# The first memory value panel of a two-block transformer kernel, in four pieces instead of two at the start of the second attention

## The reference

```python
h = x @ w_in[l]
o_a = mla_mixer(cq, ckv, kr, ...)          # 8 heads, latent attention, causal
o_b = nsa_mixer(nq, kc, vc, ks, vs, kw, vw, gl, ...)
#     8 heads, three branches: 15 compressed keys, selected blocks, window
x = layer_norm(ALPHA * x + concat([o_a, o_b]) @ w_out[l], ...)
k, v = split(memn @ xa_wkv[l], 2)          # memory keys and values, 256 x 1024 each
x = layer_norm(ALPHA * x + softmax(q @ k.T) @ v @ xa_wo[l], ...)
x = layer_norm(ALPHA * x + conv_ffn(x), ...)
```

## Time and profile before

| | |
|---|---|
| runs | 1833.0, 1834.21, 1839.84 us; median 1834.21 |
| the profiled execution | 1841.68 us; its span 1839.8 us |
| TensorE (PE) busy | 1771.1 us, 96% of the span |
| VectorE (DVE) | 1058.2 us, 58% |
| ScalarE (ACT) | 355.3 us, 19% |
| GpSimd (POOL) | 190.8 us, 10% |
| mean granted clock of TensorE | 0.979 of full speed |
| start of the second attention | 892.12 us in layer 1, 1421.54 us in layer 2 |

### The profile page before, as it was taken

How to read it: one execution, slowest core, us unless ns; L and a number is a source line. 1 busy time by engine, 2 the same in 40 slices (tenths; PEclk the granted TensorE clock), 3 DMA queues, 4 the chain that set the end, 5 groups by cost and what they waited for, 6 DMA issues and landing times.

```text
span 1839.8 us, 22077 instructions
## 1 busy us (share of the span) xinstructions
PE 1771.1 (96%) x8510; PEld 1307.5 (71%) x8510; DVE 1058.2 (58%) x2084; ACT 355.3 (19%) x881; POOL 190.8 (10%) x126
## 2 busy tenths in 40 slices
PE   7999999998899999999999999999999999999997
PEld 6886488744747885477694859984668766689953
DVE  6766468524654776641172158995712451369985
ACT  1111000132401111102270212220012440222210
POOL 1212212000011122120001000002110000000010
PEclk9999999999899999999989999999999899999999
DMA  9644354523066454436303435453355105164440
GB/s 319 209 138 177 120 206 135 192 102 115 8 207 198 150 178 160 161 104 194 148 15 125 138 115 168 155 182 133 138 143 203 72 1 199 52 204 154 170 160 23
DMA packets 162502, 265.59 MB, mean 144 GB/s; under 512 B 4008, under 2 KB 105684, under 8 KB 162270
## 3 DMA queue, kind: packets, MB, share of 16 engines
q1 hardware_dynamic: 157470, 248.18, 40.1%
q0 software_dynamic: 4768, 15.48, 2.5%
q10 hardware_dynamic: 160, 0.52, 0.1%
HBM read 262.56 MB, written 1.08 MB: 143 GB/s over the span
## 4 chain that ended last, share of the span: by engine, by line
PE 76%; DVE 14%; DVEq 4%; ACT 3%; issue 2%; DMA 1%; SPq 1%; ACTq 0%
PE psum L764 14%; PE psum L924 11%; PE psum L820 10%; PE psum L737 8%; PE psum L1125 5%; PE psum L1042 4%; PE psum L1077 3%; PE psum L1336 3%; PE psum L1293 3%; PE psum L714 3%; DVE work L2354 3%; PE psum L975 2%; PE psum L963 2%; DVE ring L1865 2%; PE psum L1059 2%
## 5 line engine op out<-in xcount | busy, mean ns | idle before, releaser
L608 POOL TENSOR_TENSOR work<-ring,work 128x1024 f32<-128x1024 f32 (+1 forms) x57 | 141.4, 2482 | 809.5 <-DVE work L1867 809.5
L924 PE MATMUL psum<-ring,work 128*128 128x512 f32 x352 | 161.9, 595 | 3.4 <-DVE work L2387 3.4
L1863 DVE TENSOR_TENSOR work<-ring 128x1024 f32<-128x1024 f32 (+1 forms) x83 | 100.7, 1213 | 86.6 <-PE psum L924 80.8
L737 PE MATMUL psum<-ring,x_t 128*128 128x512 f32 x320 | 140.0, 595 | 7.4 <-ACT x_t L1394 7.4
L924 PEld LDWEIGHTS psum<-ring,work 128*128 128x128 f32 x352 | 66.5, 190 | 85.0 <-issue 79.9
L924 PE MATMUL psum<-work 128*128 128x512 f32 x264 | 123.3, 596 | 0.0
L737 PEld LDWEIGHTS psum<-ring,x_t 128*128 128x128 f32 x320 | 60.0, 190 | 81.5 <-issue 71.8
L2007 DVE CUSTOM_DVE_ANT_0 work<-psum,work 128x256 f32<-128x256 f32 (+1 forms) x96 | 31.3, 364 | 131.2 <-PE psum L1042 131.2
L1865 DVE TENSOR_TENSOR ring<-ring 128x1024 f32<-128x1024 f32 (+1 forms) x83 | 102.3, 1232 | 6.2
L1867 DVE TENSOR_TENSOR work<-ring 128x1024 f32<-128x1024 f32 (+1 forms) x83 | 99.6, 1200 | 6.2
L924 PEld LDWEIGHTS psum<-work 128*128 128x128 f32 x264 | 50.1, 192 | 63.1 <-issue 61.4
(11 more groups left out here) (252 smaller groups left out, 2899.5 us busy)
## 6 DMA issues: line engine op xcount, KB each, us to landing
ring<-in_ffn_w_up_dram SPq DMA_DIRECT2D x66, 1024.0 KB, 7.9
ring<-in_w_in_dram SPq DMA_DIRECT2D x21, 2048.0 KB, 7.9
ring<-in_ffn_w_down_dram SPq DMA_DIRECT2D x20, 2048.0 KB, 7.8
ring<-in_ffn_w_gate_dram SPq DMA_DIRECT2D x22, 1024.0 KB, 5.5
ring<-in_xa_wkv_dram SPq DMA_DIRECT2D x8, 2048.0 KB, 7.9
ring<-in_w_out_dram SPq DMA_DIRECT2D x6, 2048.0 KB, 8.7
ring<-in_xa_wq_dram SPq DMA_DIRECT2D x4, 2048.0 KB, 7.8
ring<-in_xa_wo_dram SPq DMA_DIRECT2D x4, 2048.0 KB, 9.6
```

What stands on the lines that cost most here:

```text
L608: nc.gpsimd.tensor_tensor(t4, quarters(n, chunks, pitch)[2], t2, ALU.subtract).then_inc(fourth_ready, 1)
L737: return mm(bank(banks[2 * i + h]), acts[:, c, i * P:(i + 1) * P], ring[:, (n0 + c // 4) % RING, o:o + 512], start=(c == 0), stop=(c == KD ...
L924: last = mm(sums[p], acts[p][:, q, :], rhs[:, i, :], start=(q == 0), stop=(q == KF // 2 - 1))
L1863: v.tensor_tensor(t3, b22, b12, ALU.subtract)
```

## The change

The same sixteen products are issued in four groups of four: tile 0 with k = 0 to 3 before the scores of unit 1, tile 0 with k = 4 to 7 before those of unit 2, and tile 1 likewise before those of units 3 and 4. The wait of `keys_out` now stands ahead of the first group. `start` and `stop` still hold at k = 0 and k = 7, so an accumulation stays open in its bank while other banks are written. `panel_done` is raised by the last group, and ScalarE copies the two banks at its step 5.

```diff
-                def memory_values(j, tiles, banks):
+                def memory_values(j, tiles, banks, chunks=range(KD)):
 
                     n = at(L_WV[j], N_LAYER, l)
-                    if 0 in tiles:
+                    if 0 in tiles and 0 in chunks:
                         arrived(n)
                     for i in tiles:
-                        for k in range(KD):
+                        for k in chunks:
                             last = mm(bank(banks[i]), MEMT[:, k, i * P:(i + 1) * P], ring[:, n % RING, k * 512:k * 512 + 512],
                                       start=(k == 0), stop=(k == KD - 1))
-                    if 1 in tiles:
+                    if 1 in tiles and KD - 1 in chunks:
                         last.then_inc(panel_done, 1)
 
-                def keys_out():
-                    pe.wait_ge(group_free, at(H_WK + 2, G_LAYER, l))
-
-                def first_values():
-                    memory_values(0, (0,), (1, 3))
-
-                def second_values():
-                    memory_values(0, (1,), (1, 3))
+                def values_between(i, half):
+
+                    def between():
+                        if (i, half) == (0, 0):
+                            pe.wait_ge(group_free, at(H_WK + 2, G_LAYER, l))
+                        memory_values(0, (i,), (1, 3), range(4 * half, 4 * half + 4))
+                    return between
...
-                attend(UNITS_2, U1, l, {1: keys_out, 2: first_values, 3: second_values})
+                attend(UNITS_2, U1, l, {1 + 2 * i + h: values_between(i, h) for i in range(TT) for h in range(2)})
...
-                attend(UNITS_2, U1, l, {4: lambda: memory_values(0, (1, 3), 2)})
+                attend(UNITS_2, U1, l, {5: lambda: memory_values(0, (1, 3), 2)})
```

## The result

| | before | after |
|---|---|---|
| median of 16 runs each | 1835.09 us | 1825.21 us |
| lowest and highest | 1828.43, 1844.35 | 1816.31, 1830.6 |
| the profiled execution | 1841.68 us | 1828.62 us |
| its span | 1839.8 us | 1826.8 us |
| mean granted clock in it | 0.979 | 0.988 |

The ratio of the run times is 0.9937, with a 95% interval of 0.992 to 0.9955: the kernel is 0.6% faster. The chain of waits has not changed its shape (compare): TensorE is still 76% of it.

The account below looks back on a forecast made before the run. TensorE, 76% of the chain of waits, was taken as the bound. 6.2 + 1.7 + 4.0 + 1.5 - 2.0 = 11.4 us, 2.0 less in a median run, gave 9.4 off 1834.21: 1824.8 us, range 1818 to 1834.5.

Parts of the forecast that it names:

- First fall: Scores of units 0 and 1 and first half panel, both layers: parting the scores keeps the clock full; 6.2 us gained.
- The wait and the values behind it: Before and in unit 2's turn and unit 1's values: fourth group covers the wait, 1.7 us; clock stays full, 4.0 us.
- Units 5 to 13: Start of attention proper, both layers: VectorE and ScalarE set 1.51 us per unit at full clock; 1.5 us gained.
- Against it: Thin work after third and fourth groups: one clock fall in two layers and a little of a second; 2.0 us lost.
- From one execution to the median: Whole run: a median run has shorter clock falls than the profiled one, so the gain is 2.0 us less.
- Costs of nothing: Around the groups: earlier panel and keys' copy, later scores, panel copy one step on and next load cost nothing.
- the first: Moved stretch, both layers: clock holds throughout, gain 11.4 to 13.4 us, time 1821 to 1823; chance 0.22.
- Rival 3: Same stretch: slow time only moves, only the wait's 1.7 us is gained, 1832.5 us; chance 0.11.
- Rival 4: Panel pieces run at 1.2 GHz, each 3.43 us dearer; with five slow, 10 us slower, 1844; chance 0.07.

Follow-up runs that it names:

- e4: Kernel before plus four redundant products per layer between the scores of units 0 and 1: 1838.38 against 1838.01 us, ratio 1.0005.
- e8: The change measured again with no edit: 1822.98 us, ratio 0.9929 to the kernel before.
- e5: The change with ScalarE's panel copy at step 4 instead of 5: ratio 0.9932 to the kernel before.
- e10: The change with groups of 1, 7, 4 and 4 products before units 1 to 4: 1826.19 us, ratio 0.9945 to the kernel before.
- e3: The change regrouped as two groups of eight, before the scores of units 1 and 4: ratio 0.9984 to the kernel before.
- e9: The change with groups of 2, 6, 4 and 4 products before units 1 to 4: 1822.11 us, ratio 0.9924 to the kernel before.
- e7: The change with 4, 2, 3, 3 products before units 1 to 4, one each before 6, 8, 10, 12, copy at step 17: 1816.98 us, ratio 0.9901.

## Why the prediction was right

The mechanism was the forecast one. That the time is met to 0.5 us is in part luck, as the last two terms show. Step by step, measured in the profiled executions:

- **First fall**, 6.2 us expected. Scores 0 to 2 took 13.97 and 13.95 us before (892.12 to 906.09 in layer 1) and 10.94 after: 6.0. The clock held, as forecast, and e4 shows that it is the clock. The first two groups took 3.63 and 3.54 us from start to start instead of the 3.43 I took, and the scores of a unit 1.89 instead of 2.0.
- **The wait and the values behind it**, 1.7 + 4.0 us expected. From the scores of unit 2 to those of unit 5 it was 16.90 us (906.09 to 922.99) and 17.02; it is 14.30 in both: 5.3. In each layer the fourth group is 0.1 us longer than 3.43, and the turn of unit 2 takes 0.31 us instead of 0.22. The prediction's words that the clock falls "not after idleness" are shown for the first fall only; the second came right behind a wait.
- **Units 5 to 13**, 1.5 us expected, 2.8 measured (12.95 and 12.73 against 11.28 and 11.63). This term was mis-sized. I took VectorE's pace of 1.51 us for all eight units, but the first ones run at TensorE's 1.1 to 1.2 us until the other engines are the ones behind.
- **Against it**, 2.0 us expected for a fall left over. This term was mis-sized too. There was one fall in the profiled execution, in layer 2, but it met units 6 and 7 and not a piece of the panel. It cost nothing that can be read: layer 2's stretch takes 36.87 us with it and 36.86 in e8 without.
- **From one execution to the median**, 2.0 us expected. The profiled execution of before lies 6.6 us over the median of its kernel (1841.68 against 1835.09), that of the change 3.4 over its own (1828.62 against 1825.21): 3.2 us. Why is open. I put it down to shorter falls in this stretch in a median run, and no trace of a median run of before shows them.
- **Costs of nothing.** The two that were measured held: there is no wait before piece 1, and the copy's place is free (e5).

So 13.4 - 2.0 - 2.0 = 9.4 us was forecast, and what was measured is 14.1 in the two stretches, less 1.1 in the rest of the program and 3.2 from execution to median, which is 9.9 but for rounding. The gain in the stretches was put 2.7 us too low, and what had to come off it again 2.3 too low. The two errors cancel.

Of the rivals, the first (the clock holds throughout, 11.4 to 13.4 us) is nearest to the traces; the forecast was nearest in the medians. Rival 3 (the slow time only moves) is excluded by the table by stretch and by e4. Rival 4 (pieces at 1.2 GHz) did not come about with four or two products in a piece, but its mechanism exists: e10 is it, with one. The rule of the Trainium skill that I set against the change (TensorE: Matmul & The Clock Gate, section "HAM oscillation — how this bites in real kernels": dense products in one run keep the engine warm) did not decide this case. On that page the advice stands against waits on DMA, and TensorE waited on none in this stretch. The thin products have to be run anyway, and e3 against the change (39.9 to 36.5 us) shows that dense work does more when it is dealt out between them. What the Trainium skill says on the cause (same page, section "What's actually happening"), that the clock follows how busy TensorE has been, agrees with e4. But TensorE was shown busy for all of the 3.06 us ahead of the first fall, so a stretch shown full in a profile is no sign that the clock will hold.

## What to carry to other kernels

Look at the granted clock beside the timeline wherever small products stand in a row: if a dense group behind them has records of twice the length, deal some dense work that has no deadline out between the small products. Little was needed here: two products of 128x512 between the two groups of scores were enough in e9's trace, and one was not in e10's. Even redundant products nearly paid for themselves (e4). What was left of the dense work went best into steps in which another engine set the pace, in pieces no longer than two steps' slack (e7). And compare the same stretch with and without a fall before you give a fall a price: one of 3.42 us, just ahead of units in which VectorE and ScalarE set the pace, cost nothing.

## What the runs showed that was not expected

The scatter between executions of one kernel goes with the clock. Of the 16 runs of the change, the slowest two (1830.56 and 1830.6 us) had a mean granted clock of 0.986, and the fastest three (1816.31, 1816.6 and 1817.17) 0.996. So 1% of mean clock went with some 14 us between them, more than the whole change gives. The change's two traces differ in the same way far from the products that were moved: from 1170 to 1400 us the granted clock was 0.98 in the first and 1.00 in e8's, with the same instructions. And the same order of products met the clock differently from one place to another: after 2.70 to 3.06 us of thin products it fell in the kernel before, while e3 kept 1.00 through 8.34 us of thin work, with waits in it, before it fell. One trace of such a stretch is a sample, and a term read from one layer of one trace can be off by as much as the forecast's leftover fall was.
